# Decode attention and the wait order of a YOCO decoder step on one core: broadcast query rows, page values by VectorE, squares summed in PSUM, turns ahead of fills

## The chip, the cores and the metric

The kernel runs on one core of one Trainium2 chip. The metric is device microseconds of one execution; the median of three runs of the kernel before is 3066.99 us (3066.74 to 3067.17). The profile is one further execution, recorded by the hardware profiler.

## The reference

One inference step of a two-layer decoder for two request groups that share weights: a prompt of 1024 new rows and 8 decode rows, each with 256 cached keys and values in two pages of 128. Layer 0 is a gated linear recurrence and a SwiGLU network, then one shared K/V is projected, and layer 1 is differential attention over it and a second SwiGLU. The parts that the change touches, cut:

```python
def shared_kv(h, kv_norm, w_kv):
    k, v = jnp.split(rmsnorm(h, kv_norm) @ w_kv, 2, axis=-1)
...
def diff_combine(s, lam, valid):
    p = jax.nn.softmax(jnp.where(valid, s, -jnp.inf), axis=-1)
    return p[:, :, 0] - lam * p[:, :, 1]

def diff_attn_sample(q, k_new, v_new, k_past, v_past, lam, rel_bias):
    s = jnp.concatenate([jnp.einsum('bqhcd,bkhcd->bhcqk', q, k_past),
                         jnp.einsum('bqhcd,bkhcd->bhcqk', q, k_new)], axis=-1) * scale
    s = s + rel_bias_for(rel_bias, q_pos, k_pos)[None, :, None]
    a = diff_combine(s, lam, k_pos[None, :] <= q_pos[:, None])
    return (jnp.einsum('bhqk,bkhv->bqhv', a[..., :P], v_past)
            + jnp.einsum('bhqk,bkhv->bqhv', a[..., P:], v_new))
...
# layer 1: o = rmsnorm(diff_attn, subln_b) * (1 - lam_init); x += o @ w_out_b; x += swiglu_ffn(rmsnorm(x))
```

There are 4 attention heads of two halves of 128 channels. Everything is float32.

## The kernel before

Activations lie feature-major: 8 chunks of 128 channels by 1032 columns (1024 prompt columns, then 8 decode columns). A weight product is three float32r matmuls, since both sides are split into a high and a low part (`split_product`, L648 to L650). Weights come in slabs of 1 MB over one staging tile `w_stage`; GpSimd makes `w_hi` (L610) and `w_lo` (L612) of each slab in one of two slots, for the key/value and query slabs after a product with a gain (L607). A slab's split needs its slot back, which TensorE reports by `retire`. The split of the next slab can't start before its DMA has landed, and that DMA is issued only after the split before it.

The engines run programs written out by hand and meet at semaphores; nothing is scheduled by a planner.

**Norm before the K/V stage** (`add_pair` with `norm_ph == "kv"`): VectorE adds the last down products to the residual (L1961), 24 adds of 344 columns in PSUM banks 6 and 7, and between them makes low parts (`out_rest`, L1779) and sums of squares (`sum_square`, L1774). TensorE's first slab of queries takes one low part per chunk and waits for all the squares at chunk 4 (`norm_sum`, L664).

**Prompt attention**, 32 items (head h, block n of 128 queries). Per item TensorE does: scores of the next item (`at_scores`, L1067), some groups of the K/V projection with the turn of the group before (`kv_fill`: L648 to L650, then `kv_turn`, L1045), values of the item before (L1087), the turn of this item's weights (L1077), more groups, and last the turns of finished rows of the head before (`at_turn_rows`, L1097). Two tables, `FILL_A` (ahead of the values) and `FILL_B` (behind the weight turn), say which groups stand where, `LATE_ROWS` and `LAST_ROWS` which rows. Turns of chunks and of rows share PSUM bank 2, which ScalarE copies out. ScalarE also makes the exponentials (L1541) and copies the turned weights (`a_tok`, L1552), without which the scores two items on can't start. VectorE scales rows (L2080), makes logits, maxima and weights.

**Decode and output projection** (`wob`): 24 groups, w = 0 to 15 of 384 prompt columns, then 8 of 264 columns that hold the decode columns too. Between them stands the decode attention. `dq_spread(b)` (L1135) spreads query b over all partitions by 8 matmuls, ScalarE copies the result to `d_q_all` (L1633), VectorE multiplies two key pages with it (L2137) and sums one half (L2142), ScalarE the other (L1641). Key pages are double buffered; SyncE fetches page pair b once query b-2 is scored. After w = 8 TensorE turns the scores (`d_logits`, L1144), the softmax follows, after w = 10 the weights are turned, and after w = 11 and w = 13 `d_values` (L1172) multiplies value pages as stationary operand with one column each: 128 matmuls. After w = 15 comes the norm of the decode rows, whose high and low parts (L2203) group 16 needs. VectorE adds each group to the residual (`wob_add`, L2150); three PSUM banks are in rotation.

**Norm before the last SwiGLU**: squares of 1032 columns are summed in SBUF (L1774), low parts are L1791.

## Time and profile before

| what | value |
|---|---|
| median of the runs shown | 3066.99 us |
| profiled execution, its own time | 3068.63 us |
| its span | 3066.8 us |
| TensorE matmul / weight load | busy 2871.7 us (94%) / 2783.2 us (91%) |
| VectorE / ScalarE / GpSimd | 1322.3 (43%) / 585.0 (19%) / 956.9 us (31%) |
| mean granted TensorE clock | 0.96 of full |
| chain that ended last, by engine | PE 85%, DVE 8%, issue 3%, ACT 2%, POOL 1% |

The profiled execution took 1.8 us more than its span and 1.6 us more than the median. A share of busy time is a mean over stages: both SwiGLU stages hold TensorE at 100%, and what is idle lies in the stretches between. The stages by time: recurrence to about 760 us, first SwiGLU 800 to 1560, queries to 1680, prompt attention to 2088, decode and output projection to 2287, second SwiGLU to 3030.

### The profile page before, as it was taken

The numbers are of one execution on the slowest core, as the hardware profiler recorded it, in microseconds if no ns is written. First come the engines' busy times: TensorE is split into PE (matmuls) and PEld (weight loads), VectorE is DVE, ScalarE is ACT, GpSimd is POOL, SyncE is SP. The second block draws the span as 40 slices with busy tenths as digits, with TensorE's granted clock in tenths as the row PEclk, the third lists the DMA queues.
The fourth block names the chain that finished last, engine by engine and source line by source line (L and its number), as shares of the span: only waits on it lengthen the run. The fifth ranks groups of instructions, "written<-read, shape, count | busy, mean of one in ns | idle before, by whom it ended". The sixth has DMA issues, their size and how long they took to land.

```text
span 3066.8 us, 43328 instructions
## 1 busy us (share of the span) xinstructions
PE 2871.7 (94%) x17949; PEld 2783.2 (91%) x17949; DVE 1322.3 (43%) x2077; ACT 585.0 (19%) x1157; POOL 956.9 (31%) x270
## 2 busy tenths in 40 slices
PE   4999999989899999999989989878969999999998
PEld 3999999989899999999979778757969999999998
DVE  6345555544533333333451554555153333333335
ACT  3122222221300000000120233334031000000003
POOL 3322332213243333433435320221143333433431
PEclk7999999989999999999999999988789999999999
DMA  3111111131111111111121111124311111111111
GB/s 97 35 43 50 50 50 50 47 104 39 42 42 56 42 47 51 42 55 42 56 91 49 51 38 38 46 70 157 119 43 56 42 52 45 42 56 42 42 55 56
DMA packets 201069, 170.82 MB, mean 56 GB/s; under 512 B 6154, under 2 KB 184957, under 8 KB 200894
## 3 DMA queue, kind: packets, MB, share of 16 engines
q1 hardware_dynamic: 160576, 134.30, 14.2%
q10 hardware_dynamic: 40318, 33.92, 3.4%
q8 instruction: 143, 2.34, 0.3%
q14 instruction: 32, 0.26, 0.0%
HBM read 142.86 MB, written 25.33 MB: 55 GB/s over the span
## 4 chain that ended last, share of the span: by engine, by line
PE 85%; DVE 8%; issue 3%; ACT 2%; POOL 1%; PEld 0%; ACTq 0%; DMA 0%; SPq 0%; DVEq 0%; PEldq 0%; POOLq 0%
PE ps L648 24%; PE ps L650 23%; PE ps L649 23%; PE ps L843 3%; PE ps L1067 3%; PE ps L1087 2%; PE ps L1172 2%; DVE hg_k L1846 1%; DVE rstd L1774 1%; DVE act_lo L1779 1%; DVE stats L2047 1%; DVE hg_q L1845 1%; DVE act_lo L1791 1%; PE ps L1135 1%; DVE act_whole L1731 1%
## 5 line engine op out<-in xcount | busy, mean ns | idle before, releaser
L648 PE MATMUL ps<-act_hi,w_hi 128*128 128x344 f32 (+2 forms) x3840 | 1262.8, 329 | 55.4 <-DVE act_lo L1757 15.2
L649 PE MATMUL ps<-act_lo,w_hi 128*128 128x344 f32 (+2 forms) x3840 | 1238.0, 322 | 0.0
L650 PE MATMUL ps<-act_hi,w_lo 128*128 128x344 f32 (+2 forms) x3840 | 1237.5, 322 | 0.0
L610 POOL TENSOR_TENSOR w_hi<-w_stage,ones 128x2048 fp32r<-128x2048 f32 (+1 forms) x105 | 383.4, 3651 | 1654.8 <-PEq L698 1607.1
L648 PEld LDWEIGHTS ps<-act_hi,w_hi 128*128 128x128 f32 x3840 | 733.0, 191 | 66.7 <-issue 43.1
L649 PEld LDWEIGHTS ps<-act_lo,w_hi 128*128 128x128 f32 x3840 | 732.6, 191 | 4.7 <-issue 3.0
L650 PEld LDWEIGHTS ps<-act_hi,w_lo 128*128 128x128 f32 x3840 | 731.9, 191 | 0.0
L612 POOL TENSOR_TENSOR w_lo<-w_stage,w_hi 128x2048 fp32r<-128x2048 f32 (+1 forms) x105 | 488.2, 4650 | 8.3
L1961 DVE TENSOR_TENSOR resid<-resid,ps 128x344 f32<-128x344 f32 x528 | 270.1, 513 | 190.4 <-PE ps L650 189.8
L648 PE MATMUL ps<-h_hi,w_hi 128*128 128x344 f32 x1056 | 340.5, 322 | 10.0 <-DVE resid L1961 10.0
L649 PE MATMUL ps<-h_lo,w_hi 128*128 128x344 f32 x1056 | 338.9, 321 | 0.0
L650 PE MATMUL ps<-h_hi,w_lo 128*128 128x344 f32 x1056 | 338.3, 320 | 0.0
L1938 DVE TENSOR_TENSOR ps<-ps,rstd 128x344 f32<-128x344 f32 x132 | 68.9, 525 | 384.9 <-PE ps L650 384.9
L1941 DVE TENSOR_TENSOR ps<-ps,rstd 128x344 f32<-128x344 f32 x132 | 69.2, 524 | 363.3 <-PE ps L650 363.3
L1483 ACT ACTIVATE silu_gate<-ps 128x344 f32<-128x344 f32 x132 | 60.4, 458 | 811.1 <-DVE ps L1938 811.1
L648 PEld LDWEIGHTS ps<-h_hi,w_hi 128*128 128x128 f32 x1056 | 199.2, 189 | 13.1 <-DVE resid L1961 12.9
L649 PEld LDWEIGHTS ps<-h_lo,w_hi 128*128 128x128 f32 x1056 | 199.8, 189 | 0.0
L650 PEld LDWEIGHTS ps<-h_hi,w_lo 128*128 128x128 f32 x1056 | 199.5, 189 | 0.0
L1488 ACT CAST h_hi<-ps 128x344 fp32r<-128x344 f32 x132 | 59.0, 447 | 445.8 <-DVE ps L1944 445.8
L843 PEld LDWEIGHTS ps<-hg_q,hg_k 128*128 128x128 f32 x896 | 110.5, 199 | 26.2 <-DVE hg_k L1846 25.5
L843 PE MATMUL ps<-hg_q,hg_k 128*128 128x64 f32 x896 | 113.1, 281 | 21.4 <-DVE hg_k L1846 21.4
L1067 PE MATMUL ps<-k_feat,q_all 128*128 128x512 f32 (+3 forms) x192 | 81.1, 565 | 27.9 <-ACT a_tok L1552 27.3
(257 smaller groups left out, 2291.3 us busy)
## 6 DMA issues: line engine op xcount, KB each, us to landing
w_stage<-in_w_gate_up SPq DMA_DIRECT2D x88, 512.0 KB, 5.0
w_stage<-in_w_down SPq DMA_DIRECT2D x44, 512.0 KB, 4.1
w_stage<-in_w_in_a SPq DMA_DIRECT2D x32, 512.0 KB, 5.2
w_stage<-in_w_kv SPq DMA_DIRECT2D x16, 512.0 KB, 4.4
k_page<-in_cache_k SPq DMA_DIRECT2D x16, 512.0 KB, 4.4
v_page<-in_cache_v SPq DMA_DIRECT2D x16, 512.0 KB, 4.7
w_stage<-in_w_out_b SPq DMA_DIRECT2D x12, 512.0 KB, 4.5
x_spill<-resid ACTq DMA_DIRECT2D x8, 516.0 KB, 2.7
```

The lines of the kernel that those rows point to most:

```text
L610: g.tensor_tensor(WH[s][:, 0:cols], WST[:, 0:cols], ones[:, 0:1].to_broadcast([P, cols]), ALU.mult).then_inc(w_hi, 1)
L612: g.tensor_tensor(WL[s][:, 0:cols], WST[:, 0:cols], WH[s][:, 0:cols], ALU.subtract).then_inc(w_split, 1)
L648: pe.matmul(out, wh, xh, start=first, stop=False)
L649: pe.matmul(out, wh, xl, start=False, stop=False)
L650: return pe.matmul(out, wl, xh, start=False, stop=last)
L843: last = pe.matmul(PS[:, 3 + l % 2, c * 64:(c + 1) * 64], K[h % 2][:, c * P:(c + 1) * P], q[:, c, :, 1, :], start=True, stop=True)
L1067: last = pe.matmul(PS[:, bank + k0 // 512, 0:k1 - k0], QA[:, 2 * h + c, n * P:(n + 1) * P], KTB[h % 2][:, c, k0:k1], start=True, stop=True)
L1087: last = pe.matmul(PS[:, 7, 0:256], AT[:, j, :], VTOK[h % 2][:, j, :], start=(j == 0), stop=(j == n))
L1172: last = pe.matmul(PS[:, 7, m * DEC + b:m * DEC + b + 1], VPG[b % 4][g][:, m * P:(m + 1) * P], DAS[:, g, r:r + 1], start=(g == 0), stop=(g ...
L1938: v.tensor_tensor(PS[:, t, 0:TS], PS[:, t, 0:TS], RS[:, tile(t)], ALU.mult).then_inc(ffn_gscaled, 1)
L1941: v.tensor_tensor(PS[:, 3 + t, 0:TS], PS[:, 3 + t, 0:TS], RS[:, tile(t)], ALU.mult).then_inc(ffn_uscaled, 1)
L1961: v.tensor_tensor(X[:, m, tile(t)], X[:, m, tile(t)], PS[:, 6 + q % 2, 0:TS], ALU.add).then_inc(ffn_down_free, 1)
```

## The change

It has six parts.

1. **Queries by DMA.** Eight transposes after the second K/V group turn the decode queries into rows; ScalarE copies them to SBUF and stores them in DRAM. SyncE broadcasts row b to all partitions (`query`, 512 KB), behind the two key pages of b. `dq_spread` and `dq_copy` are gone.
2. **Page values.** VectorE multiplies each page by its weights per head (`page_values`: 4 `tensor_scalar` and 4 `scalar_tensor_tensor` of 128x256 for each query), and TensorE sums over the tokens with a selector `pick` of 8 columns as the stationary operand: 2 matmuls of 512 columns each, 16 in all, into rows 0 to 7 of banks 3 and 4. ScalarE copies the rows, 8 transposes turn them back.
3. **Places.** `d_logits` moves from behind w = 8 to behind w = 4, the weight turn from 10 to 6, the values from 11 and 13 to 8 to 13. SyncE issues slabs 3 and 4 of the output projection behind value pages 3 and 7.
4. **Attention.** Turns of rows stand behind the scores (`ROWS_A`) or behind the weight turn (`ROWS_B`), one row at a time, always ahead of the fills; group 11 of each head moves from `FILL_B` of item 3 to `FILL_A` of item 4, and the slab's `retire` in item 4 from ahead of the fills to behind the weight turn.
5. **Squares.** Before the last SwiGLU the prompt's squares are summed in PSUM banks 6 and 7; those of the decode columns by one reduction.
6. **GpSimd and order.** The split of the second slab of `ffn0`, `kv` (queries) and `ffn1` waits for all 8 low parts of that norm. In the K/V norm low parts come three chunks late, sums of squares behind the adds.

```diff
-        LATE_ROWS = [(), (0, 1)] + [(n,) for n in range(2, NB)]
-        LAST_ROWS = [(), (0, 1, 2), (3, 4, 5), (6, 7), (), (), (), ()]
-        FILL_A = [(4,), (6,), (8,), (10,), (), (12,), (13,), (15,)]
-        FILL_B = [(5,), (7,), (9,), (11,), (), (), (14,), ()]
+        ROWS_A = [(), (), (1,), (), (), (), (), ()]
+        ROWS_B = [(), (0,), (2,), (3,), (4,), (5,), (6,), (7,)]
+        LAST_ROWS_A = [(), (), (1,), (3,), (5,), (7,), (), ()]
+        LAST_ROWS_B = [(), (0,), (2,), (4,), (6,), (), (), ()]
+        FILL_A = [(4,), (6,), (8,), (10,), (11,), (12,), (13,), (15,)]
+        FILL_B = [(5,), (7,), (9,), (), (), (), (14,), ()]
...
+            def query(b):
+                sp.dma_start(QBC[b % 2][:].rearrange("p m n -> p (m n)"),
+                             bass.AP(q_rows.tensor, b * D, [[0, P], [1, D]])).then_inc(dq_in[b % 2], 16)
...
+            sp.wait_ge(at_turned, AH * NB + OPENED)
+            query(0)
+            query(1)
+            sp.wait_ge(at_av_full, AH * NB + OPENED)
+            sp.wait_ge(v_out[1], 16 * 12)
             for b in range(2, DEC):
                 sp.wait_ge(pg_scored, b - 1 + OPENED)
                 pages(kc, KPG, k_page_in, b, b % 2)
+                query(b)
...
+                if n in (S_F0 + 1, S_Q + 1, S_F1 + 1):
+                    pool.wait_ge(operand_split, hi_before("ffn0" if n < S_Q else "kv" if n < S_F1 else "ffn1") + C)
                 pool.wait_ge(w_staged, n * 32 + 32)
...
+            def d_value(b):
+                pe.wait_ge(v_summed, b + 1)
+                for u in range(2):
+                    last = pe.matmul(PS[0:DEC, 3 + u, :], pick[:, 7 - b:15 - b], VPG[b % 4][0][:, 512 * u:512 * (u + 1)],
+                                     start=(b == 0), stop=(b == DEC - 1))
+                last.then_inc(pv_full, 1)
...
-            dq_spread(0)
-            dq_spread(1)
+            pe.wait_ge(at_o, AH * NB + OPENED)
             for w in range(24):
                 wob_group(w)
-                if w < 6:
-                    dq_spread(w + 2)
+                if w == 4:
+                    d_logits()
+                elif w == 6:
+                    d_turn_weights()
                 elif w == 8:
-                    d_logits()
+                    d_new_rows(0)
+                    d_value(0)
+                elif w == 9:
+                    d_value(1)
                 elif w == 10:
-                    d_turn_weights()
-                elif w == 11:
-                    for b in range(4):
-                        d_values(b)
+                    d_new_rows(1)
+                    d_value(2)
+                elif w in (11, 12):
+                    d_value(w - 8)
                 elif w == 13:
...
-                        if norm_ph == "kv" and m:
-                            out_rest("kv", m - 1, X[:, m - 1, :])
-                        if norm_ph == "kv" and m in (3, 5):
-                            sum_square("kv", m // 2)
+                        if norm_ph == "kv" and m > 2:
+                            out_rest("kv", m - 3, X[:, m - 3, :])
...
+            def page_values(b):
+                slot = VPG[b % 4]
+                dve.wait_ge(v_page_in[b % 4], 32 * (b // 4 + 1))
+                for h in range(AH):
+                    part = slice(256 * h, 256 * (h + 1))
+                    last = v.tensor_scalar(slot[0][:, part], slot[0][:, part], DAS[:, 0, h * DEC + b:h * DEC + b + 1], None, ALU.mult)
+                last.then_inc(v_scaled, 1)
...
+            def sum_prompt(c):
+                dve.wait_ge(norm_sq, NB + (nth("ffn1") - 1) * C + c + 1)
+                dve.wait_ge(norm_acc, nth("ffn1") * (C - 1) + c - 1)
+                v.tensor_tensor(total if c + 1 < C else RS[:, 0:SEQ], total, SQ[:, (c - 1) % SQN, 0:SEQ], ALU.add).then_inc(norm_acc, 1)
```

TensorE between the weight turns of items 3 and 4 of head 1, before. `v_feat` is a turn of a K/V chunk, `q_all` under L1097 a turn of rows, `k_feat` scores, `v_rows` values, `probs` the weight turn; the K/V group 11 stands ahead of this piece.

```order
L1045 MATMUL ps<-ident,v_feat_120 128x128 x2
L1097 MATMUL ps<-ident,q_all 128x128 x2
L1067 MATMUL ps<-k_feat_118,q_all 128x512
L1067 MATMUL ps<-k_feat_118,q_all 128x256
L1067 MATMUL ps<-k_feat_118,q_all 128x512
L1067 MATMUL ps<-k_feat_118,q_all 128x256
L1087 MATMUL ps<-v_rows_119,a_tok 128x256 x4
L1077 MATMUL ps<-ident,probs 128x128 x5
L1097 MATMUL ps<-ident,q_all 128x128 x2
L1067 MATMUL ps<-k_feat_118,q_all 128x512
```

The same engine from the weight turn of item 3 on, in the changed kernel.

```order
L1108 MATMUL ps<-ident,probs 128x128 x4
L1128 MATMUL ps<-ident,q_all 128x128 x2
L1098 MATMUL ps<-k_feat_119,q_all 128x512
L1098 MATMUL ps<-k_feat_119,q_all 128x256
L1098 MATMUL ps<-k_feat_119,q_all 128x512
L1098 MATMUL ps<-k_feat_119,q_all 128x256
L679 MATMUL ps<-act_hi,w_hi_56 128x264
L680 MATMUL ps<-act_lo,w_hi_56 128x264
```

Before, a group stood between the weight turn of item 3 and the scores, and none between those scores and the values; now it is the other way round.

VectorE around the logits of the decode rows, before: page products (`d_k_times_q`), the adds of output groups (`resid`), then the logits.

```order
L2137 TENSOR_TENSOR d_k_times_q_146<-k_page_136,d_q_all_148 128x1024
L2142 TENSOR_REDUCE d_scores_tok<-d_k_times_q_145 128x4x2
L2150 TENSOR_TENSOR resid<-resid,ps 128x384 x2
L2165 COPY d_stats<-lam 32x1
L2150 TENSOR_TENSOR resid<-resid,ps 128x384
L2169 SCALAR_TENSOR_TENSOR d_logits<-ps,d_bias 64x257
```

The same place in the changed kernel, and below the first page values behind the add of group 8.

```order
L2175 TENSOR_TENSOR d_k_times_q_148<-k_page_137,d_q_all_150 128x1024
L2180 TENSOR_REDUCE d_scores_tok<-d_k_times_q_147 128x4x2
L2218 COPY d_stats<-lam 32x1
L2221 SCALAR_TENSOR_TENSOR d_logits<-ps,d_bias 64x257
```

```order
L2204 TENSOR_TENSOR resid<-resid,ps 128x384
L2239 TENSOR_TENSOR d_t_164<-v_sample,d_a_new_sum 128x4x8 x2
L2188 TENSOR_SCALAR v_page_138<-v_page_138,d_a_sum 128x256 x4
L2193 SCALAR_TENSOR_TENSOR v_page_138<-v_page_139,d_a_sum,v_page_138 128x256 x4
L2188 TENSOR_SCALAR v_page_140<-v_page_140,d_a_sum 128x256 x4
L2193 SCALAR_TENSOR_TENSOR v_page_140<-v_page_141,d_a_sum,v_page_140 128x256 x4
```

Three adds no longer stand between the last page product and the logits, and 64 page instructions are new behind them.

## Rows read from the trace of the kernel before

**Rows 1.** TensorE's waits, 1690 to 2088: line, releaser, total us, times, longest.
```profile
PE ps L1067 <- ACT a_tok L1552: 27.3, 11, 4.5
PE ps L1097 <- DVE q_all L2080: 10.4, 7, 6.8
PE ps L1097 <- issue: 5.1, 8, 0.8
PE ps L1097 <- ACT v_rows L1532: 3.2, 5, 0.7
```

**Rows 2.** TensorE's waits, 2088 to 2310.
```profile
PE ps L648 <- POOL w_lo L612: 10.6, 2, 6.5
PE ps L648 <- DVE act_lo L1791: 8.9, 1, 8.9
PE ps L648 <- issue: 5.5, 1, 5.5
PE ps L648 <- DVE act_lo L2203: 4.7, 1, 4.7
```

**Rows 3.** Timeline of the K/V norm: start us, duration us, what, idle before.
```profile
1544.32 0.66 PE L648 MATMUL ps<-h_hi,w_hi 128*128 128x344 f32 x1 [4.17 <-DVE resid L1961]
...
1578.97 2.07 PE L664 MATMUL ps<-rstd,ones 128*128 128x512 f32 x2 [6.10 <-DVE rstd L1774]
...
1538.71 3.98 DVE L1779 TENSOR_TENSOR act_lo<-resid,act_hi 128x1032 fp32r<-128x1032 f32 x1
...
1569.13 9.78 DVE L1774 TENSOR_TENSOR rstd<-rstd,squares 128x1032 f32<-128x1032 f32 x5
...
1538.00 3.60 POOL L607 TENSOR_TENSOR w_stage<-w_stage,vectors 128x2048 f32<-128x2048 f32 x1 [5.93 <-DMA w_stage<-in_w_q_b]
```

**Rows 4.** Timeline of head 1, items 3 to 6, ScalarE and TensorE.
```profile
1818.89 0.57 ACT L1552 COPY a_tok<-ps 128x512 f32<-128x512 f32 x1
...
1831.15 5.90 PE L1067 MATMUL ps<-k_feat,q_all 128*128 128x512 f32 x8 [3.84 <-ACT a_tok L1552]
...
1845.72 3.67 PE L1067 MATMUL ps<-k_feat,q_all 128*128 128x512 f32 x8 [1.23 <-ACT a_tok L1552]
```

**Rows 5.** Stretches: us, busy of PE, PEld, DVE, ACT, POOL, granted clock, DMA.
```profile
2208.00:2212.00 4.00, 4.00 (x21) 4.00 (x20) 0.00 (x0) 0.00 (x0) 0.00 (x0) 0.50 0.00 0
```

**Rows 6.** Timeline of the page scores, VectorE and GpSimd, 2088 to 2150.
```profile
2093.74 2.36 DVE L2137 TENSOR_TENSOR d_k_times_q<-k_page,d_q_all 128x1024 f32<-128x1024 f32 x2 [5.24 <-issue]
...
2102.64 2.36 DVE L2137 TENSOR_TENSOR d_k_times_q<-k_page,d_q_all 128x1024 f32<-128x1024 f32 x2 [3.02 <-ACT d_k_times_q L1641]
...
2128.82 7.80 DVE L2137 TENSOR_TENSOR d_k_times_q<-k_page,d_q_all 128x1024 f32<-128x1024 f32 x2 [1.89 <-ACT d_k_times_q L1641]
...
2139.24 2.36 DVE L2137 TENSOR_TENSOR d_k_times_q<-k_page,d_q_all 128x1024 f32<-128x1024 f32 x2 [0.90 <-ACT d_k_times_q L1641]
...
2144.42 2.36 DVE L2137 TENSOR_TENSOR d_k_times_q<-k_page,d_q_all 128x1024 f32<-128x1024 f32 x2 [1.10 <-DMA k_page<-in_cache_k]
...
2130.07 5.47 POOL L612 TENSOR_TENSOR w_lo<-w_stage,w_hi 128x2048 fp32r<-128x2048 f32 x1
```

**Rows 7.** Timeline of VectorE around the values and for prices of its instructions.
```profile
2198.31 0.55 DVE L2150 TENSOR_TENSOR resid<-resid,ps 128x384 f32<-128x384 f32 x1 [3.60 <-PE ps L650]
2222.15 0.22 DVE L2191 TENSOR_TENSOR d_o<-d_t,ps 128x64 f32<-128x64 f32 x1 [23.29 <-PE ps L1172]
...
2156.47 4.52 DVE L2177 TENSOR_SCALAR d_diag<-ident,d_logits 64x64 f32<-64x64 f32 x1
...
2081.99 2.19 DVE L2080 TENSOR_SCALAR q_all<-q_all,row_factor 128x256 f32<-128x256 f32 x8 [5.23 <-ACT row_factor L1568]
...
1806.94 0.75 DVE L2061 SCALAR_TENSOR_TENSOR probs<-probs,stats 128x512 f32<-128x512 f32 x1
```

**Rows 8.** Groups by line and shape, TensorE, 2088 to 2310.
```profile
L1172 PE MATMUL ps<-d_a_sum,v_page 128*128 128x1 f32 x256 | 46.5, 319 | 0.0
L1135 PE MATMUL ps<-ident,q_sample 128*128 128x128 f32 x128 | 17.4, 296 | 0.7 <-ACT q_all L1575 0.7
```

212 lines of the change are left out of this document (122 added, 90 removed).

## The prediction

> **What bounds the kernel now.** I read the waits of TensorE by stage first, since its busy share is near full in both SwiGLU stages and a gain can only come from stretches where it waits, runs at the lower clock, or does work that can go. In the prompt attention [rows 1] the scores wait 27.3 us for the copied weights, 11 times, and the turns of rows 18.7 us in three rows, of which 6.8 us is the one wait at the very end (for the row factor, after the last item). In the decode stretch [rows 2] it waits 5.5 us before the first output group, 4.7 us for the low part of the decode rows, 10.6 us for two weight splits and 8.9 us for the first low part of the last norm. Then the timelines show what a wait costs beside itself: the scores that follow the 3.84 us wait take 5.90 us for 1792 columns, the next ones after 1.23 us only 3.67 us for 2048 [rows 4]. And the page values run at granted clock 0.50, the 1.2 GHz level, with TensorE 100% busy [rows 5]: 128 matmuls of one column take 46.5 us [rows 8].
>
> **K/V norm.** The split of the second query slab now waits for all low parts, its L607 with it. Before, that L607 stood at 1538.00 and the low part at 1538.71 took 3.98 us [rows 3] instead of the 1.2 us that its unhindered neighbours need; the adds came late and TensorE idled 4.17 us, with other waits of 2.5, 1.4 and twice 0.3 us near it, and restarted at the low clock. Two low parts at m = 1 and 3 that ran into GpSimd are moved to where it is quiet. In the changed kernel five low parts lie among the adds and cost 0.3 us each, and no sum does. The 18 adds from m = 2 on then take 18 x 0.945 + 1.4 = 18.4 us from 1529.8, so the adds end at 1548.2 instead of 1559.3. Not all of that is kept. TensorE waits at chunk 4 for the sums (6.10 us) [rows 3], and these are now a tail of VectorE: one sum, three low parts and six sums (10 x 1.23 = 12.3 us), with the whole split (3.6 + 3.6 + 4.6 = 11.8 us) let loose in the middle of it. End 1548.2 + 12.3 + 11.8 = 1572.3 against 1578.9. **Gain 6.6 us**; bounds 3 (a second slab's L607 gets in too) and 11 (all). At the first SwiGLU's norm the same gate moves 9 us of blocking from low parts to sums that TensorE awaits equally: 0, bounds -1 and +1.
>
> **Prompt attention.** (a) Turns of rows. Waits of 3.6 (10.4 less 6.8), 5.1 and 3.2 us [rows 1], 11.9 in all, come from the one bank that chunk turns and row turns share. One turn at a time behind scores or the weight turn finds the bank copied out, and the next chunk turn stands a whole group (4.15 us) later. I leave 1.5 us: gain 10.4, bounds 6 and 12 (13 with a slow stretch behind three turns in head 3). (b) Group 11. It leaves the place behind the weight turn of item 3, so the next scores there must wait for ScalarE's copy: in head 1 that copy ended at 1819.5 [rows 4], the weight turn at 17.3 and a row turn at 17.6, a new wait of 2.0 us. It fills the place ahead of item 4's values, but logits, maximum, exponentials, now also a chunk's copy and DMA issue on ScalarE, and the weight copy still take some 10.7 us from those scores to the next ones (before 9.7). Scores at 1819.6 + 10.7 = 1830.3 instead of 1831.15. So 3.84 us turns into about 2.0 and 2.3, gain 0.5 in the sum of four heads. (c) What is worth more is the clock behind it: 5.90 us would be some 3.3 at the rate of the next row, four times 2.2 us, 9 us. A wait of 1.23 us left the clock alone, one of 3.84 did not; two of about 2 us lie between. I take half, 4.5, bounds 0 and 9. (d) The eight query turns at the start cost 1.0 us of TensorE; copy, store and reading back are hidden behind the 20 and more us until the first page, the two first broadcasts behind the end of attention, since the bank of probabilities is free at the last weight turn and the first product begins 18 us later. **Gain 14.4 us**, bounds 4 and 21.
>
> **Decode stretch to group 16** (2238.88 before, which is the wait of 4.7 us for the low part). Removed: spreads of 17.4 us, of which eight matmuls each for two queries lay in idle time, and values of 46.5 us [rows 8]. But the chain through VectorE decides, so I walk it.
> - The first product need not wait 5.24 us for a spread query [rows 6]: it starts at 2088.6, the last low parts end at 2094.6, and groups start there instead of 2099.7.
> - The second product stood 8.9 us behind the first [rows 6]: 2098. From then on product, ScalarE's sums, product: 5.2 us apart where no copy lay between (2139.24 to 2144.42), taken as 5.1, since each query's load (two pages, then a third DMA) lands some 7 us after its release and 3.6 us of scoring follow, 5.4 us per query at the worst. GpSimd's split of slab 2 meets the products again; it cost 7.80 - 2.36 = 5.4 us, because a product waited for the whole L612 [rows 6]. Last product 2098 + 6 x 5.1 + 5.4 = 2134, both halves summed by 2140 (before: logits at 2149.7).
> - `d_logits` now stands behind w = 4. Five groups are done by 2094.6 + 5 x 4.15 + 1.6 = 2117, where one group takes 0.55 + 3.60 us [rows 7]. **TensorE idles 23 us there**, where it idled none, and starts again at the low clock. What had been done in that time, groups 5 to 8, comes after it: 2140 + 4 x 4.15 + 4.9 (logits, weight turn, turn of new rows, slow clock) = 2161.5.
> - Page values. One query costs VectorE 4 x 0.27 (eight such took 2.19 us) and at most 4 x 0.48 (0.75 us for twice the columns) [rows 7], 2.9 us. The first meets the split of slab 3, which its `retire` lets go 3 us before group 8 ends: two-input and even small one-input instructions waited for a whole L612 (`d_diag`, 64x64, 4.52 us) [rows 7]. It is ready at about 2170.5, a wait of 9 us for TensorE. After it VectorE has 2.9 us of work per 4.15 us group and is ahead.
> - Then 7 groups (29.1), 16 matmuls of 512 columns with 8-column weights at 3.67 / 4 = 0.9 us (14.4) [rows 4], turns, slow clock and sums 4.2: 2170.5 + 47.7 = 2218.2. Plus 4.7: 2222.9. **Gain 16 us**, bounds 6 (broadcasts slower by 2 us each) and 30 (neither split is met).
>
> Slab 3, issued later, lands at about 2148 and is needed at 2158; slab 4 lands at 2201, needed at 2231: nothing for either unless values slip by 30 us.
>
> The SBUF page is worth weighing here. The trace first: several of the times above are VectorE waiting out a GpSimd instruction. The Trainium skill, "SBUF — State Buffer", section "SBUF: two separate sides", says the pair of ports that both engines use is an exclusive lock for the whole instruction, against two-input VectorE instructions and those in a two-port mode, and that the loser fully blocks. It speaks against this change: all 64 page instructions are of these kinds, while the matmuls they replace were not. Without that rule the time would be 9 us lower; by it, and by the rows, the 9 us stand in the sum.
>
> **Last norm.** The slabs' chain (split, DMA, split) sets 2238.9 to 2286.7, not the sums. But three L612 took 5.4 us instead of 4.6 since a sum slipped in between (5.47 in [rows 6] is the same effect). Sums with one operand in PSUM do not do that: 2 us. Low parts without a split beside them (16.2 us for seven before) save TensorE 1 us in the first slab. **Gain 3 us**, bounds 1 and 4. Two more memsets stand in GpSimd's chain that TensorE awaits at the start: a loss of 0.3 us.
>
> **Sum.** 6.6 + 14.4 + 16 + 3 - 0.3 = 39.7 us. Against the span of 3066.8 us that gives 3027.1; the median of the runs is 0.2 us above the span: 3027 us.
>
> **Rivals.**
> 1. Turns ahead give nothing: the waits for copied weights [rows 1] grow by what the turns lose, and new waits of 2 us pull the clock down in items 3 and 4. Attention at +1 instead of +14.4: 3040. For it: those waits are the larger ones; against it: they lie in items 4 to 7, the turns' waits in items 1 to 3 too. Chance 0.15.
> 2. VectorE meets no split in the page chain and the clock holds in attention: 3027 - 12 - 5 = 3010, or 3006 with all of the K/V norm's. Chance 0.14.
> 3. Slower than before. One mechanism: the broadcast, 128 reads of one 4 KB row of DRAM, behind both pages in one queue. No row shows such a load. Six of them lie in the chain of products, where TensorE already waits; each us beyond 7 from release to landing costs half to all of 6 us. To lose 40 us each must land 14 us after its release; at 16 us the time is about 3076. Loads of the same size landed in 3.4 to 6.6 us, so chance 0.05.
> 4. Page values become the bound: every one of the eight waits for a split or a late page, 4 us each, and TensorE drops to the low clock between them: 3027 + 25 = 3052. Only one split lies in that stretch, so chance 0.08. With the tail of rival 1 it comes within 0.2% of before (0.04).
>
> **How the numbers follow.** Forecast 0.54, over 3017 to 3035; the rivals as given. What a measurement can tell from no change is about 0.2%, 6 us: faster (below 3061) 0.54 + 0.15 + 0.14 + 0.08 = 0.91, taken as 0.90 since the sum leaves something out in most cases; same 0.04; slower 0.06. Range 3004 to 3049: it holds forecast and rivals 1 and 2, and the near part of 4, and the ends are the bounds of the parts taken two at a time.
>
> **What would show it.** Right: products of pages about 5 us apart and the first at 2088 less what is gained before; a TensorE wait of 20 us or more in front of the transposes of scores, a second of some 9 us before the first selector matmul, granted clock 1.00 through the values; row turns without waits; the K/V sums ending 6 to 7 us sooner. Wrong: no wait at the logits, or one over 35 us; key pages or queries as releaser of most products; the scores of item 5 still near 5.9 us in each head. If the stretch up to group 16 isn't shortened by 6 to 30 us, the sum is wrong whatever the total says.

## The result, and the profile after

The changed kernel takes 3029.99 us (median of four executions, 3020.9 to 3033.6) against 3066.86 us, a ratio of 0.9877 (95% interval 0.9854 to 0.99). The profiled execution took 3033.57 us, its span is 3031.8 us. The forecast was 3027 us with a range of 3004 to 3049. Of 39.7 us in the sum, 36.9 came by the medians and 35.0 by the spans. The profile of "queries ahead", further down, is of an execution of 3192.91 us at a granted clock of 0.83, a slower state that some executions fall into, and no time of it is used.

The first reading is by stage, from one event to the next, since totals of 3030 us hide which term was right. "Control" is the unedited changed kernel profiled again in the experiments.

| From ... to (TensorE) | before | after | control | gain by after | forecast |
|---|---|---|---|---|---|
| start ... sums of the first SwiGLU's norm | 804.72 | 801.21 | 797.77 | 3.5 | -0.3 |
| ... sums of the K/V norm | 774.25 | 768.15 | 768.59 | 6.1 | 6.6 |
| ... first of the last row turns | 503.43 | 489.90 | 487.31 | 13.5 | 14.4 |
| ... decode group 16 | 156.48 | 147.64 | 147.35 | 8.8 | 16 |
| ... first low part of the second SwiGLU | 47.86 | 46.77 | 46.20 | 1.1 | 3 |
| ... end | 780.06 | 778.13 | 777.48 | 1.9 | 0 |

The attention answers to [rows 1] with its waits of TensorE from 1668 to 2066 us (line, releaser, total, times, longest):

```profile
PE ps L1098 <- ACT a_tok L1597: 21.0, 15, 2.5
PE ps L1128 <- DVE q_all L2119: 9.7, 4, 6.9
PE ps L1128 <- ACT k_rows L1569: 6.9, 6, 1.8
...
PE ps L1128 <- ACT v_rows L1577: 3.3, 4, 1.2
...
PE ps L1128 <- issue: 0.5, 2, 0.2
```

One row of the kernel before belongs beside them, in the window of [rows 1]:

```profile
PE ps L1097 <- ACT k_rows L1524: 1.4, 2, 0.7
```

The scores' waits for copied weights fell from 27.3 to 21.0 us, the longest from 4.5 to 2.5 us. The row turns' waits did not fall. Before, they were 10.4 + 5.1 + 3.2 + 1.4 = 20.1 us, now they are 9.7 + 6.9 + 3.3 + 0.5 = 20.4 us. Those for issue are nearly gone, and in their place stands `k_rows`: in item 1 of heads 1 to 3 a row turn comes right behind a chunk turn and waits 1.83 us for the copy out of the bank that both share. That wait was not in the sum.

The decode stretch answers to [rows 2] (2066 to 2290 us):

```profile
PE ps L1173 <- ACT d_k_times_q L1683: 28.2, 1, 28.2
PE ps L679 <- POOL w_lo L643: 10.4, 2, 7.1
PE ps L679 <- DVE act_lo L1830: 7.4, 1, 7.4
PE ps L1201 <- DVE v_page L2193: 7.2, 1, 7.2
```

The large new wait is the one in front of the turns of scores, L1173. The K/V norm answers to [rows 3], in a timeline (start us, duration us, engine, idle before):

```profile
1550.86 18.45 DVE L1813 TENSOR_TENSOR rstd<-rstd,squares 128x1032 f32<-128x1032 f32 x6
...
1551.02 4.53 POOL L638 TENSOR_TENSOR w_stage<-w_stage,vectors 128x2048 f32<-128x2048 f32 x1 [22.67 <-DVE act_lo L1818]
...
1560.18 5.37 POOL L643 TENSOR_TENSOR w_lo<-w_stage,w_hi 128x2048 fp32r<-128x2048 f32 x1
```

The split waits 22.67 us for the last low part and then runs into six sums, which take 18.45 us. TensorE's wait there grew from 6.10 to 10.53 us, and still the sums end 6 us sooner. What fell are its waits for the adds, first before, then after (line, releaser, total, times, longest; 1515 to 1582 us of each):

```profile
PE ps L648 <- DVE resid L1961: 8.7, 5, 4.2
...
PE ps L679 <- DVE resid L2000: 1.1, 4, 0.3
```

The page scores answer to [rows 6], in VectorE's timeline of the products of keys and queries (one row is the two products of a query):

```profile
2065.39 2.36 DVE L2175 TENSOR_TENSOR d_k_times_q<-k_page,d_q_all 128x1024 f32<-128x1024 f32 x2
2074.30 2.36 DVE L2175 TENSOR_TENSOR d_k_times_q<-k_page,d_q_all 128x1024 f32<-128x1024 f32 x2 [3.03 <-ACT d_k_times_q L1683]
2080.25 2.36 DVE L2175 TENSOR_TENSOR d_k_times_q<-k_page,d_q_all 128x1024 f32<-128x1024 f32 x2 [2.17 <-DMA d_q_all<-q_sample_rows]
...
2092.41 9.38 DVE L2175 TENSOR_TENSOR d_k_times_q<-k_page,d_q_all 128x1024 f32<-128x1024 f32 x2 [2.98 <-DMA d_q_all<-q_sample_rows]
...
2117.97 2.36 DVE L2175 TENSOR_TENSOR d_k_times_q<-k_page,d_q_all 128x1024 f32<-128x1024 f32 x2 [3.01 <-DMA d_q_all<-q_sample_rows]
```

Before, such products waited for ScalarE or for a page, the first for issue. Now five of eight wait for the broadcast query, 11.6 us in all, and one is held up by a weight split (9.38 instead of 2.36 us). Each broadcast from the third on stands behind two pages in the queue. The queue's row for the third query, and the landing times of the stretch from 2060 to 2240 us (KB, median us from issue to landing):

```profile
2069.81 1.46 SPq L546 DMA_DIRECT2D k_page<-in_cache_k  x2
2071.32 0.43 SPq L558 DMA_DIRECT2D d_q_all<-q_sample_rows  x1
...
k_page<-in_cache_k SPq DMA_DIRECT2D x12, 512.0 KB, 4.4
d_q_all<-q_sample_rows SPq DMA_DIRECT2D x6, 512.0 KB, 6.3
```

The loads for the third query were released at 2069.81, and its product began at 2080.25, after 10.4 us. That is the longest of the five: the others took 6.7, 7.8, 7.1 and 9.2 us from the first page's issue to the product, 8.3 us in the mean. Two reloads of the residual (`x_spill`, 516 KB each), issued by ScalarE at 2070.17 and 2071.30, were in flight beside the longest alone. Each release came 4.3 to 4.4 us after the start of a product. Last, the values, in the place of [rows 7] and [rows 8]:

```profile
2145.77 4.50 POOL L643 TENSOR_TENSOR w_lo<-w_stage,w_hi 128x2048 fp32r<-128x2048 f32 x1
...
2145.70 4.61 DVE L2239 TENSOR_TENSOR d_t<-v_sample,d_a_new_sum 128x32 f32<-128x32 f32 x2
2150.34 1.14 DVE L2188 TENSOR_SCALAR v_page<-v_page,d_a_sum 128x256 f32<-128x256 f32 x4
2151.52 1.67 DVE L2193 SCALAR_TENSOR_TENSOR v_page<-v_page,d_a_sum,v_page 128x256 f32<-128x256 f32 x4
```

One query costs VectorE 1.14 + 1.67 = 2.8 us (forecast 2.9), and ahead of the first stand two instructions of 32 columns that wait out a weight split, 4.61 us. In the kernel before the same two took 0.3 us.

### The profile page after: what moved, and what is told of

It reads as the page before. It is cut to its first block, busy times and chain, and to the rows that moved or that the text cites. A ratio compares the mean times of both kernels' runs of the same rounds, so it can differ in the third digit from the quotient of the medians.

```text
span 3031.8 us, 42717 instructions
## 1 busy us (share of the span) xinstructions
PE 2818.2 (93%) x17613; PEld 2719.4 (90%) x17613; DVE 1323.1 (44%) x2142; ACT 578.4 (19%) x1152; POOL 953.9 (31%) x272
## 4 chain that ended last, share of the span: by engine, by line
PE 82%; DVE 10%; issue 3%; ACT 2%; POOL 1%; DMA 1%; PEld 0%; ACTq 0%; SPq 0%; DVEq 0%; PEldq 0%; POOLq 0%
PE ps L679 24%; PE ps L681 23%; PE ps L680 23%; PE ps L874 3%; PE ps L1098 2%; DVE rstd L1813 1%; PE ps L1118 1%; DVE hg_k L1885 1%; DVE stats L2086 1%; DMA d_q_all<-q_sample_rows 1%; DVE probs L2100 1%; ACT probs L1586 1%; DVE d_k_times_q L2175 1%; DVE act_lo L1818 1%; DVE hg_q L1884 1%
## 5 line engine op out<-in xcount | busy, mean ns | idle before, releaser
L655 POOL TENSOR_TENSOR state_sample<-state_sample,hg_f 128x1024 f32<-128x1024 f32 x8 | 16.0, 1996 | 258.4 <-DMA state_sample<-in_state_hgrn 258.4
```

## Experiments

Twelve kernels, in three groups of four. Kernels of one group ran on one chip beside the kernel before, whose medians there were 3065.07, 3069.69 and 3066.49 us. Across groups I compare ratios to it or stretches of the traces.

### The changed kernel again

> The changed kernel again, unedited, as the measure for the others and for its own spread: executions lay between 3020.9 and 3033.6 us. Theory A (the spread is in which scores of the attention's items 4 and 5 run at the lower granted clock, and in the recurrence): again 3020 to 3034, and its four heads show 5.9 us or 3.7 us scores in another mix than before. Theory B (the spread comes from the chip as a whole): every stage is shorter or longer by the same share.

3027.68 us (3026.44 to 3029.92), ratio 0.9883 (0.9867 to 0.99). The attention's stretch is 2.6 us shorter than in the profile of after. The scores of item 5 in heads 0 and 1 show why. First after, then the control (TensorE, heads 0 and 1 of each):

```profile
1723.17 4.94 PE L1098 MATMUL ps<-k_feat,q_all 128*128 128x512 f32 x8 [2.45 <-ACT a_tok L1597]
...
1819.79 4.94 PE L1098 MATMUL ps<-k_feat,q_all 128*128 128x512 f32 x8 [1.25 <-ACT a_tok L1597]
```

```profile
1720.45 3.25 PE L1098 MATMUL ps<-k_feat,q_all 128*128 128x512 f32 x8 [2.45 <-ACT a_tok L1597]
...
1815.40 3.25 PE L1098 MATMUL ps<-k_feat,q_all 128*128 128x512 f32 x8 [1.25 <-ACT a_tok L1597]
```

The waits are equal to 0.01 us and the same scores take 4.94 or 3.25 us. After had two such rows, the control none, and that is theory A. Six of the other profiles below have the mix of after in item 5: 4.94 us in heads 0 and 1, 3.25 us in heads 2 and 3. The stretch up to the first SwiGLU's sums, whose TensorE work the change leaves alone, ended between 793.9 and 803.8 us in the profiles of the changed kernel and its variants. The spread arises in the recurrence, whose last matmuls began between 715.2 and 725.1 us (at 725.3 in the kernel before). So the 3.5 us that after shows there say nothing of the change.

### Attention as before

```
-        ROWS_A = [(), (), (1,), (), (), (), (), ()]
-        ROWS_B = [(), (0,), (2,), (3,), (4,), (5,), (6,), (7,)]
...
-        FILL_A = [(4,), (6,), (8,), (10,), (11,), (12,), (13,), (15,)]
-        FILL_B = [(5,), (7,), (9,), (), (), (), (14,), ()]
+        ROWS_A = [()] * 8
+        ROWS_B = [(), (0, 1)] + [(n,) for n in range(2, NB)]
...
+        FILL_A = [(4,), (6,), (8,), (10,), (), (12,), (13,), (15,)]
+        FILL_B = [(5,), (7,), (9,), (11,), (), (), (14,), ()]
...
+                for g in fills(FILL_B, h, n):
+                    kv_fill(g)
...
                 for m in rows_b(h, n):
                     at_turn_rows((h - 1) * NB + m)
-                for g in fills(FILL_B, h, n):
-                    kv_fill(g)
```

> The changed kernel with the order of the attention as before: row turns behind the fills of an item, group 11 behind the weight turn of item 3, the last chunk turn in item 4. Theory (the turns ahead of the fills and the clock behind them gave the 13.5 us that the two traces differ by): the last row turns end 12 to 15 us later and the time is 12 to 15 us above the control. Rival (part of it is run-to-run clock, part came from the eight query turns moved to the start): only 6 to 9 us above it. Second rival: the waits that it brings back are paid anyway in waits for copied weights, under 4 us.

3038.78 us (3037.13 to 3043.88), ratio 0.992 (0.9904 to 0.9937): 11.1 us above the control, 1 us short of the theory and above both rivals. From the K/V sums to the last row turns it takes 503.66 us, and it was 503.43 before the change: the whole 13.5 us come back in this stretch. Behind it this kernel is 3.2 us shorter than the control, where, among other things, its page products lose 5.0 us to a split and the control's 6.8. The waits are those of [rows 1] again:

```profile
PE ps L1098 <- ACT a_tok L1595: 27.3, 11, 4.5
PE ps L1128 <- DVE q_all L2115: 9.8, 6, 7.0
...
PE ps L1128 <- issue: 5.8, 9, 0.8
```

With 3.2 us for `v_rows` and 1.4 us for `k_rows` the row turns wait 20.2 us here and 20.4 us in after, so their own waits gave nothing. The gain lies in the scores. Their waits are 6.3 us shorter in after, and their own time is shorter too. The same 192 matmuls, in this kernel and then in after (stretch, us, busy of PE and PEld, granted clock, DMA):

```profile
1668.00:2076.00 408.00, 81.54 (x192) 37.98 (x192) 0.94 0.17 56
...
1668.00:2066.00 398.00, 73.53 (x192) 34.51 (x192) 0.96 0.18 58
```

They take 8.0 us less at the higher granted clock. The run undoes three edits together (the place of the row turns, group 11, the last chunk turn), and which of them spares the scores no run separates.

### Without the gates on GpSimd

```
-                if n in (S_F0 + 1, S_Q + 1, S_F1 + 1):
-                    pool.wait_ge(operand_split, hi_before(...) + C)
```

> The changed kernel without the three waits that hold back GpSimd's second weight split of the first SwiGLU, the query projection and the second SwiGLU until all low parts are made; the order of the adds and low parts stays. Theory (the gate gives most of the K/V norm's 6 us, and nothing in the two other norms): the first group behind the K/V sums starts 4 to 6 us later, the time is 4 to 7 us above the control. Rival (the order of low parts gave it, or the tail of sums meets the split either way): within 2 us of the control. For the first SwiGLU's norm, which ended 3.5 us sooner after the change: with the gates as cause it ends 1 us or less later from its last sum on; if the 3.5 us came from the recurrence, whose instructions are the same, nothing changes there.

3030.28 us (3023.59 to 3035.76), ratio 0.9891 (0.9871 to 0.9912), not to be told from the control. Between the two norms' sums 769.53 us, 0.9 to 1.4 above the kernels with the gate. VectorE and GpSimd in the K/V norm:

```profile
1541.59 3.61 POOL L639 TENSOR_TENSOR w_hi<-w_stage,ones 128x2048 fp32r<-128x2048 f32 x1 [6.42 <-PEq L727]
1545.27 5.48 POOL L641 TENSOR_TENSOR w_lo<-w_stage,w_hi 128x2048 fp32r<-128x2048 f32 x1
...
1533.87 2.39 DVE L1816 TENSOR_TENSOR act_lo<-resid,act_hi 128x1032 fp32r<-128x1032 f32 x1
...
1541.81 4.46 DVE L1816 TENSOR_TENSOR act_lo<-resid,act_hi 128x1032 fp32r<-128x1032 f32 x1
1546.20 5.63 DVE L1811 TENSOR_TENSOR rstd<-squares 128x1032 f32<-128x1032 f32 x1
...
1555.19 11.20 DVE L1811 TENSOR_TENSOR rstd<-rstd,squares 128x1032 f32<-128x1032 f32 x6
```

The split runs earlier and costs a low part 1.2, another 3.2 and the first sum 4.4 us. But in the new order TensorE's waits for the adds are still only 2.3 us in all, and the six sums that follow take 11.20 us instead of 18.45. The theory falls: beside the new order the gate mostly moves the blocking.

### The K/V norm's order as before, gates kept

```
-                        if norm_ph == "kv" and m > 2:
-                            out_rest("kv", m - 3, X[:, m - 3, :])
+                        if norm_ph == "kv" and m:
+                            out_rest("kv", m - 1, X[:, m - 1, :])
+                        if norm_ph == "kv" and m in (3, 5):
+                            sum_square("kv", m // 2)
...
```

> The changed kernel with the adds, low parts and sums of the K/V norm in the order of before, and with GpSimd's gates kept (the run without gates lost only 1 us there). Theory (the order gave the K/V norm's 6 us: no low part or sum waits for a split inside the adds): from the first SwiGLU's norm to the K/V norm's sums 4 to 6 us more than the 768.2 to 768.6 us of the runs that have the new order. Rival (either the gate or the order alone is enough, since with the gate no split meets the adds): under 2 us more.

3027.46 us (3024.53 to 3029.71), ratio 0.9876 (0.9861 to 0.9891). The stretch is 770.96 us, 2.4 to 2.8 above the others; before the change it was 774.25. So with the order alone 1 us of the gain is missing, with the gate alone some 2.5, and with neither 6. The two are largely substitutes, between the theory and the rival and nearer to the rival; the total doesn't resolve either.

### Queries read once

```
                 pages(kc, KPG, k_page_in, b, b % 2)
-                query(b)
...
-                dve.wait_ge(dq_in[b % 2], 16 * (b // 2 + 1))
+                dve.wait_ge(dq_in[b % 2], 16)
```

> Leaves out part of the computation: only the first two query rows are broadcast, and the pages of the other six are multiplied by these two. So it gives the chain of page products without six of the 512 KB broadcasts. Theory (the broadcasts behind the pages are why the logits came 5 us later than in my sum; VectorE waited 11.6 us for d_q_all): the last product starts 7 to 10 us sooner, TensorE's wait at the logits is 18 to 21 us instead of 28, the time 5 to 9 us below the control. Rival (the pages themselves land no sooner, and what is gained is lost at the weight split of slab 3): page waits of 1 to 2 us a query take the place, the time within 3 us of the control.

3018.3 us (3013.78 to 3025.76), ratio 0.9846 (0.9829 to 0.9862): 9.4 us below the control. The kernel leaves out the loads of six of the eight queries. VectorE's products:

```profile
2092.24 2.36 DVE L2174 TENSOR_TENSOR d_k_times_q<-k_page,d_q_all 128x1024 f32<-128x1024 f32 x2 [0.92 <-DMA k_page<-in_cache_k]
2097.48 7.09 DVE L2174 TENSOR_TENSOR d_k_times_q<-k_page,d_q_all 128x1024 f32<-128x1024 f32 x2 [1.17 <-DMA k_page<-in_cache_k]
```

They stand 5.0 to 5.3 us apart, which is the pace of my sum (5.1), and from the first output group to the logits it takes 43.15 us instead of 51.43 (after) and 50.97 (control). TensorE's wait at the logits is 19.9 us instead of 28.2. Of the 8 us, 2 are a cheaper meeting with the split (7.09 - 2.36 = 4.7 us against 7.0), the rest the broadcasts. What that meeting costs depends on when the two engines meet: with the same decode instructions the runs without gates and with the old attention lost 5.0 us to it, in two products.

### Queries ahead

```
+            query(2)
+            query(3)
             for b in range(2, DEC):
                 sp.wait_ge(pg_scored, b - 1 + OPENED)
                 pages(kc, KPG, k_page_in, b, b % 2)
-                query(b)
+                if b < 6:
+                    query(b + 2)
```

> All eight query rows are broadcast, but four of them into the place of the later value pages, two turns ahead of their product and no longer behind its pages. Theory (with six broadcasts left out the last product came 5 to 8 us sooner, and the wait was for their place in the queue, not for the bytes): VectorE's waits for d_q_all go, waits of 1 us a query for the pages stay, the first output group to the logits is 43 to 46 us instead of 48 to 51.4, the time 4 to 7 us below the control. Rival (the queue's bytes set the pace: 1.5 MB a query whatever the order): the waits only change their name to k_page and the stretch stays 48 to 51 us.

3018.35 us (median of the four executions that were not profiled, 3015.53 to 3022.24), ratio 0.9834 (0.9818 to 0.9851), half a per cent below the control's 0.9883, and 9 us below it by the medians. The chain of products is read from "Both", further down, whose key pages and queries are loaded in the same way:

```profile
2061.97 2.36 DVE L2178 TENSOR_TENSOR d_k_times_q<-k_page,d_q_all 128x1024 f32<-128x1024 f32 x2
...
2107.84 2.36 DVE L2178 TENSOR_TENSOR d_k_times_q<-k_page,d_q_all 128x1024 f32<-128x1024 f32 x2 [1.99 <-DMA k_page<-in_cache_k]
```

From the first product to the last it takes 45.9 us instead of 52.6, and no product waits for a query. All eight queries are loaded here too, so it was their place in the queue.

### Logits later

```
-                if w == 4:
+                if w == 8:
                     d_logits()
-                elif w == 6:
+                elif w == 10:
                     d_turn_weights()
...
+            columns(S_WOB + 3, w_out_b, 768)
             for b in range(2):
                 pages(vc, VPG, v_page_in, b, b)
...
-            columns(S_WOB + 3, w_out_b, 768)
...
```

> The turns of the scores stand behind output group 8 instead of 4, the turn of the weights behind 10, the eight values behind 11 to 13; the adds on VectorE follow, and slab 3 is loaded ahead of the value pages. Theory (TensorE's 28 us without work ahead of the logits are lost, and four groups of 4.15 us fit there): wait 10 to 13 us, groups behind the logits four fewer, the wait before decode group 16 unchanged; 10 to 17 us below the control. Rival (the chain behind the logits, weights, eight values of 2.8 us and the split of slab 3 of 8 us, sets the end, not TensorE's work): new waits of 10 us and more before the first values or before group 12, 0 to 5 us below the control.

2998.26 us (2997.65 to 2999.19), ratio 0.9768 (0.9751 to 0.9784): 29 us below the control by the medians and 35 by the ratios, nearly twice what the theory gave or more. From the logits to decode group 16 it takes 54.67 us instead of 84.11, 29.4 us less. TensorE and GpSimd:

```profile
2100.16 0.66 PE L679 MATMUL ps<-act_hi,w_hi 128*128 128x384 f32 x1 [8.87 <-DVE resid L2202]
2119.07 0.38 PE L1173 MATMUL ps<-ident,d_scores_tok 128*64 128x128 f32 x2 [0.50 <-ACT d_k_times_q L1681]
...
2117.10 3.60 POOL L641 TENSOR_TENSOR w_hi<-w_stage,ones 128x2048 fp32r<-128x2048 f32 x1 [19.89 <-DMA w_stage<-in_w_out_b]
```

One wait of 28 us became 8.87 (an add of a group queued on VectorE behind a product that a split held up) and 0.50. The wait for the first values, 7.2 us, is gone too, since the split of slab 3 began at 2117.10, while the logits were due, and not at the first values.

### Logits later, slab 3 loaded as in the change

```
-            columns(S_WOB + 3, w_out_b, 768)
             for b in range(2):
                 pages(vc, VPG, v_page_in, b, b)
...
+            columns(S_WOB + 3, w_out_b, 768)
```

The diff is against the kernel before this one.

> The kernel with the logits behind group 8, but slab 3 again loaded behind the value pages. Logits later with an early slab gained 29 us over the control, 12 more than the four groups of 16.6. Theory (the rest came from the split of slab 3, which no longer met the first values: 7.2 us of wait and its clock): with the late slab the first values or group 12 wait 8 to 12 us, and it is 10 to 14 us above the kernel with the early slab, 15 to 19 below the control. Rival (the rest is the clock and the fewer waits ahead of the logits, not the slab): under 4 us above it.

3001.8 us (3000.06 to 3011.36), ratio 0.9789 (0.9774 to 0.9804), 0.2 per cent above the early slab, which the intervals do not separate. In the profile the stretch from the last row turns to group 16 is 128.37 us against 117.96. The wait for values is back:

```profile
2143.95 6.35 PE L1201 MATMUL ps<-v_page,pick 128*8 128x512 f32 x8 [6.49 <-DVE v_page L2191]
```

So of the 29 us the later logits give 19 and the slab some 10 by the traces. But the profiled execution, 3011.36 us, was the slowest of four, and the other three took 3000.06 to 3002.93 us. The medians, from two groups, give the slab 3.5 us and the ratios 6.4, between the rival and the theory. That the late slab's split holds up the first values is shown; what it costs in most executions is not.

### Both

The edits of "queries ahead" and "logits later" together.

> Queries ahead and logits later together. Theory (two independent gains: the chain to the logits is shorter by 4 to 7, TensorE's work behind it by 16.6): 15 to 22 us below the control. Rival (each shortens the same idle time, or the splits meet the products and values again): no more than the better of the two alone, 10 to 14.

2995.05 us (2991.58 to 3001.74), ratio 0.9761 (0.9743 to 0.9779), the lowest median here. Against "logits later" it gains 3.2 us by the medians, which the spread of its executions does not resolve, and 3.3 us by the traces from the last row turns to group 16. The logits come 44.72 us behind the first output group instead of 51.02, but TensorE, no longer idle in front of them, gives back half: from the logits to group 16 57.64 instead of 54.67. The two don't add up, as the rival had it, though its 10 to 14 us below the control were far too few.

### Page values by columns

```
-                pe.wait_ge(v_summed, b + 1)
-                for u in range(2):
-                    last = pe.matmul(PS[0:DEC, 3 + u, :], pick[:, 7 - b:15 - b], ...)
+                pe.wait_ge(d_dve, D_DVE["a"])
+                pe.wait_ge(v_page_in[b % 4], 32 * (b // 4 + 1))
+                for m in range(C):
+                    for g in range(NPG):
+                        last = pe.matmul(PS[:, 7, m * DEC + b:m * DEC + b + 1], VPG[b % 4][g][:, m * P:(m + 1) * P], ...)
```

> The changed kernel with the page values as before: 128 matmuls of one column instead of 64 VectorE instructions and 16 selector matmuls, in the same places between the groups. Theory (46.5 us at the lower clock were replaced by 14.4 us and a wait of 7.2): the stretch from the first value to group 16 is 25 to 35 us longer, group 16 some 20 to 28 us later since the first value need not wait for VectorE's products, the time 20 to 28 us above the control. Rival (VectorE's way costs nearly what it saves, by the lock with the split and the later first value): under 15 us above it.

3044.47 us (3042.23 to 3051.93), ratio 0.9925 (0.9907 to 0.9942): 13 us above the control by the ratios, 16.8 by the medians, below the theory and about where the rival has it. From the logits to group 16 97.90 instead of 84.11 us. Group, then timeline:

```profile
L1204 PE MATMUL ps<-d_a_sum,v_page 128*128 128x1 f32 x256 | 34.0, 268 | 0.0
...
2141.42 3.63 PE L1204 MATMUL ps<-d_a_sum,v_page 128*128 128x1 f32 x32
...
2185.85 14.41 PE L1204 MATMUL ps<-d_a_sum,v_page 128*128 128x1 f32 x89
...
2190.00:2200.00 10.00, 10.00 (x53) 10.00 (x52) 0.00 (x0) 0.00 (x0) 0.00 (x0) 0.54 0.01 2
```

The same 128 matmuls took 46.5 us in the kernel before [rows 8] and 34.0 here. The profile has two records of each matmul, and some are missing. One query between two groups takes 3.63 us, in a stretch of granted clock 1.00. The last three in a row take 4.8 us each, and in the middle of them the granted clock is 0.54, near the 1.2 GHz level of [rows 5]. So at least 12.5 of the 46.5 us were the price of bunching them.

### Squares in SBUF

```
-                dst = SQ[:, (j - 1) % SQN, 0:SEQ] if j else PS[:, 6:8, :]...
-                a.activation(dst, X[:, (j + 4) % C, 0:SEQ], ACT.Square)
+                a.activation(SQ[:, j % SQN, :], X[:, (j + 4) % C, :], ACT.Square)...
...
-                    sum_prompt(j - 1)
+                    sum_square("ffn1", j - 1)
```

> The changed kernel with the squares of the last norm summed in SBUF by two-operand instructions of 1032 columns, as before. Theory (a sum in PSUM is not held up by a split, which the slabs' chain gains 1 to 2 us from): decode group 16 to the second SwiGLU's first group 47.3 to 48.3 us instead of 46.0 to 46.8, and the time 1 to 2 us above the control. Rival (the gate, not the squares, gave it): 46 to 46.8 as before.

3029.45 us (3025.68 to 3032.26), ratio 0.9885 (0.9869 to 0.99): not separable from the control in the total, but the stretch from group 16 to the first low part is 48.52 us instead of 46.20 (control) and 46.77 (after), the longest of all and just above the theory's range. GpSimd and VectorE:

```profile
2210.47 5.38 POOL L643 TENSOR_TENSOR w_lo<-w_stage,w_hi 128x2048 fp32r<-128x2048 f32 x1
...
2212.20 4.75 DVE L1811 TENSOR_TENSOR rstd<-rstd,squares 128x1032 f32<-128x1032 f32 x1
```

A sum with both operands in SBUF waits out the split, and the split itself takes 5.4 us three times instead of 4.5.

### Rows one item on

```
-        ROWS_A = [(), (), (1,), (), (), (), (), ()]
-        ROWS_B = [(), (0,), (2,), (3,), (4,), (5,), (6,), (7,)]
...
+        ROWS_A = [(), (), (0,), (), (), (4,), (), ()]
+        ROWS_B = [(), (), (1,), (2,), (3,), (5,), (6,), (7,)]
...
```

> Queries ahead, logits later with the early slab, and the row turn that stands behind a chunk turn in item 1 of heads 1 to 3 (TensorE waited 1.83 us there, three times, for the copy out of the shared bank) moved one item on. Theory (those waits are on the path): they go, 3 to 6 us below the kernel that has the other two (2995.1), so 2989 to 2992. Rival (an even row turn later shows up as a wait for copied weights, or lets a score run at the lower clock): within 2 us of 2995, or above.

3001.67 us (2995.64 to 3009.05), ratio 0.9789 (0.9773 to 0.9806), 7 us above "Both", the kernel without this edit. From the first scores to the last row turns it takes 395.3 us instead of 388.1:

```profile
PE ps L1133 <- ACT v_rows L1580: 10.2, 6, 3.7
...
PE ps L1133 <- ACT k_rows L1572: 1.4, 3, 0.6
```

The 1.83 us waits are gone (`k_rows` 6.9 to 1.4 us) and a new one of up to 3.7 us for `v_rows` stands in another place, so that the row turns wait 3.2 us more in all. The larger part is the scores' own time, 79.0 us instead of 73.3, at a granted clock of 0.94 instead of 0.96: the rival. The row turns of the change are better placed than mine.

## Why the prediction was right, and where it was not

**K/V norm: 6.6 forecast, 6.1 measured.** The size held, the share of its causes did not. I put the gain on the gate, with the moved low parts as a help. The runs show that the gate alone gives 3.3 us and the order alone 4.7. The adds ended 10.5 us sooner (11.1 forecast), and the tail that I expected, with the whole split in it, is there: six sums of 7.4 us take 18.45, and TensorE waits 10.53 us instead of 6.10.

**First SwiGLU's norm: 0.** The trace shows a gain of 3.5 us, but the same instructions end anywhere in a span of 10 us from one execution to the next. The loss of 0.3 us at the start is there: the first matmul began at 11.74 us instead of 11.41.

**Attention: 14.4 forecast, 13.5 measured**, and undoing it brings all of it back. The size is right by luck, since the terms behind it were wrong. Most of it, 10.4 us, was to come from the row turns' waits. They were 20.1 us before and are 20.4 after (13.3 and 13.5 without the one at the very end), and the sign "row turns without waits" did not show. The bank that both kinds of turn share made them wait in new places, three times 1.83 us for `k_rows`, and the run that removed these put other waits in their place. Group 11 was to give 0.5 us by its waits, but the scores' waits for copied weights fell by 6.3 us. The clock was to give 4.5 us, and the scores' own time fell by 8.0 us against the run with the old order. For the scores of item 5 I had four times 2.2 us and took half. Before, they took 4.94 to 5.90 us in the four heads (5.90 in the head of [rows 4]). In after they took 3.25 us in two heads and 4.94 in two, so 5.5 of 8.9 us came, and in the control all of it. The eight query turns cost 0.9 us (1.0). Rival 1 falls as to the total and as to its mechanism, since the waits for copied weights, which it had growing, fell. It was right in that the turns gained nothing by their own waits.

**Decode stretch: 16 forecast, 8.8 measured**, and this is the term that was mis-sized. Measured from the first of the last row turns, step by step: the first product came at 6.1 us (forecast 6.2), the output groups at 12.3 (12.2), the second product 8.9 us behind the first (8.9). Then the pace: from the second product to the last 43.7 us, and I had 6 x 5.1 + 5.4 = 36. Without the split, which cost 7.0 instead of 5.4 us, the pace was 36.7 / 6 = 6.1 us a query. I had taken a load to land "some 7 us after its release", with 3.6 us of scoring behind it. With two pages ahead of the query it was 8.3 us in the mean (6.7 to 10.4), and the next release came 4.4 us after a product's start. With two buffers a query then costs (8.3 + 4.4) / 2 = 6.3 us. Rival 3 named this mechanism, and its price, 3 to 6 us for each us beyond 7, gives 4 to 8 us; it came to 6.1. Without the broadcasts the pace is 5.0 to 5.3 us; with the queries ahead in the queue, in "Both", it is 5.0 to 6.1. The prediction had "key pages or queries as releaser of most products" as a sign of being wrong, and five of eight products had a query as releaser: that sign showed. From the logits on the walk held: first selector matmul after 30.3 us (30.5), then 53.7 to group 16 (52.4). The wait at the logits was 28.2 us (23), because they came later while the groups ended as forecast, and that at the values 7.2 (9). The granted clock through the values was 0.50 in their first 4 us and 0.99 behind (1.00 forecast).

What the walk saw and did not use is worth more than all its terms. It priced the idle 23 us and went on, as if the position behind group 4 were given. Moving the logits back by four groups, with slab 3 loaded sooner, took another 29 us off, beside the 37 of the change.

**Page values.** The sum put 46.5 us out and 14.4 + 9 in. The selector matmuls took 16.4 us and the wait in front of them 7.2. Undone in the changed kernel they cost 13.8 us, not 23. I took the price of 46.5 us, read at a clock of 0.50, for one of the instructions. At 3.63 us a query it would be 29 us, so more than a third of it belonged to their order.

**The rule on the shared ports** (the Trainium skill, "SBUF — State Buffer", section "SBUF: two separate sides") agrees with the trace: two instructions of 32 columns take 4.61 us beside a split. The sums with an operand in PSUM took 1.23 us throughout, those in SBUF up to 5.19.

**Last norm: 3 forecast, 1.1 measured** in the stretch (1.7 in the control), within the bounds of 1 to 4, and undoing the squares costs 1.8 to 2.3. The end behind it was 1.9 us shorter, which I had at 0 and can't explain: it was 777.5 to 779.8 us in the variants, and the kernel before was profiled only once.

The total was near because a term too large by 7 us met gains of 3.5 and 1.9 us that I had not counted, the first of which is chance, and because the attention's wrong terms added up to nearly the right sum.

## What to carry to other kernels

When a walk along a chain shows an engine idle for 20 us ahead of a fixed place in its order, ask next which of its later work could stand in front, and whether the buffers and the other engine's order allow it: this gained more than the part being judged. Price a double-buffered load with everything that is ahead of it in its queue, and put the piece that is wanted last ahead by a turn. Before a sum of waits is booked as a gain, ask what else holds the same bank: here the row turns waited as long as before, for other copies. A price per instruction that was read at a low granted clock belongs to the arrangement as much as to the instruction.

## What the runs showed of the hardware

- With equal waits ahead (1.25 us) the same scores took 3.25 or 4.94 us in the same place of two executions. The clock after a short wait is not settled by the length of that wait.
- The 16 one-column matmuls of a query take 3.63 us between groups of 384 columns, at a granted clock near 1.00. With four queries together they take 46.5 / 8 = 5.8 us each; in the stretch of [rows 5] TensorE is 100% busy at 0.50.
- A one-input instruction of 257 columns (0.41 us alone) took 3.05 us beside a split in "logits later":

```profile
2122.50 3.05 DVE L2234 TENSOR_SCALAR d_logits<-d_logits,d_stats 64x257 f32<-64x257 f32 x1
```

- Page products lost between 4.7 us ("queries read once") and 7.3 us ("logits later") to one weight split, by when they met its two halves.
- A 512 KB broadcast of one 4 KB row behind two pages landed 6.3 us after its issue (median), a page of the same size after 4.4. The first two broadcasts, with no page ahead of them, landed after 3.9 and 4.8 us.
- A sum of squares with an operand in PSUM took 1.23 us even beside a split, the one with both operands in SBUF up to 5.19 us.
